# Expert gathers by token block, a hidden gate stage for block 0, and diagonals made by ScalarE, in a two-layer hybrid encoder on one Trainium2 core

## The reference

```python
x = x + _peer(_rmsnorm(x, norm_ffn[i]), peer_wq[i], peer_keys[i], peer_u[i], peer_v[i])
gate = jax.nn.sigmoid(_rmsnorm(x, norm_ple[i]) @ ple_gate[i])
x = x + (p[i] @ ple_proj[i]) * gate
```

```python
u = jnp.take(u_tab, ex, axis=0)
act = jax.nn.gelu(jnp.einsum('thkd,td->thk', u, hx), approximate=False) * gx
vv = jnp.take(v_tab, ex, axis=0)
return jnp.einsum('thk,thkd->td', act, vv)
```

## Time and profile before

| | us |
|---|---|
| median of 3 runs | 1844.28 |
| lowest and highest of them | 1842.87, 1846.96 |
| the profiled execution's own time | 1852.54 |
| its span in the profile | 1850.7 |
| its mean granted PE clock, as a share of full speed | 0.955 |
| PE busy | 1523.7 (82%) |
| DVE busy | 1339.5 (72%) |
| ACT busy | 439.3 (24%) |
| POOL busy | 568.6 (31%) |

### The profile page before, as it was taken

How to read it: one execution, slowest core, us unless ns; L and a number is a source line. 1 busy time by engine, 2 the same in 40 slices (tenths; PEclk the granted TensorE clock), 3 DMA queues, 4 the chain that set the end, 5 groups by cost and what they waited for, 6 DMA issues and landing times. The chain is left out here.

```text
span 1850.7 us, 23157 instructions
## 1 busy us (share of the span) xinstructions
PE 1523.7 (82%) x8613; PEld 849.1 (46%) x8613; DVE 1339.5 (72%) x3171; ACT 439.3 (24%) x1145; POOL 568.6 (31%) x556
## 2 busy tenths in 40 slices
PE   8999487979787887888899993878787887978886
PEld 7987342424333333422599872424333333423224
DVE  5776887877868587866477678777868696877654
ACT  5653211202111111100366441202111111201003
POOL 0010243434343433343000102434443443334321
PEclk9999799999999999999999996989899999999998
DMA  7312599999999999999242126999999999999980
GB/s 287 115 48 104 215 390 418 410 405 424 404 405 398 422 390 427 404 426 427 114 160 98 65 93 270 397 395 421 397 427 407 424 401 427 402 410 412 427 362 34
DMA packets 83767, 604.43 MB, mean 327 GB/s; under 512 B 9296, under 2 KB 9424, under 8 KB 10704
## 3 DMA queue, kind: packets, MB, share of 16 engines
q0 software_dynamic: 73728, 536.90, 70.2%
q1 hardware_dynamic: 9936, 66.21, 9.4%
HBM read 602.03 MB, written 1.05 MB: 326 GB/s over the span
## 5 line engine op out<-in xcount | busy, mean ns | idle before, releaser
L1480 PE MATMUL PS<-gath,diag 128*128 128x512 f32 x2048 | 1005.5, 631 | 285.5 <-DVE diag L1042 284.9
L1031 DVE CUSTOM_DVE_ANT_0 gath<-gath,xn 128x1024 f32<-128x1024 f32 x512 | 626.1, 1224 | 320.2 <-DMA gath<-in_experts,idx 319.9
L370 POOL DMA_INDIRECT gath<-in_experts,idx x512 | 535.0, 1045 | 842.5 <-PE PS L1480 779.9
L1480 PEld LDWEIGHTS PS<-gath,diag 128*128 128x128 f32 x2048 | 377.5, 197 | 878.7 <-DVE diag L1042 535.0
L615 ACT ACTIVATE hgel<-hid 128x1 f32<-128x1 f32 x512 | 103.9, 203 | 1088.3 <-DVE hid L1031 1088.3
L1136 PE MATMUL PS<-hTh,high 128*128 128x256 f32 x592 | 179.1, 303 | 5.2 <-DVE hTl L691 3.5
L1042 DVE TENSOR_SCALAR diag<-cst,hgel,gate 128x128 f32<-128x128 f32 x512 | 176.0, 344 | 0.0
L674 DVE TENSOR_TENSOR low<-ring,high 128x1024 fp32r<-128x1024 f32 x110 | 133.6, 1223 | 55.9 <-ACT high L390 55.7
L1136 PE MATMUL PS<-hTh,low 128*128 128x256 f32 x592 | 166.5, 281 | 0.0
L1136 PE MATMUL PS<-hTl,high 128*128 128x256 f32 x592 | 166.5, 281 | 0.0
L390 ACT CAST high<-ring 128x1024 fp32r<-128x1024 f32 x110 | 114.5, 1046 | 31.1 <-PE PS L1152 28.9
(11 more groups left out here) (241 smaller groups left out, 1339.2 us busy)
## 6 DMA issues: line engine op xcount, KB each, us to landing
ring<-in_w_slabs SPq DMA_DIRECT2D x58, 1024.0 KB, 5.2
gath<-in_experts,idx POOLq DMA_INDIRECT x512, 10.8
xres<-in_x SPq DMA_DIRECT2D x2, 512.0 KB, 4.6
gffn<-in_gain_ffn SPq DMA_DIRECT2D x2, 512.0 KB, 5.7
out<-obuf SPq DMA_DIRECT2D x2, 512.0 KB, 2.6
cst<-in_consts SPq DMA_DIRECT2D x1, 680.0 KB, 10.9
praw<-in_p_t SPq DMA_DIRECT2D x1, 512.0 KB, 15.5
gfin<-in_g_final SPq DMA_DIRECT2D x1, 512.0 KB, 3.1
```

Source lines behind the costliest of these rows:

```text
L370: pool.indirect_dma_start(gath[:, n % NB], None, experts[L], bass.IndirectOffsetOnAxis(ap=idx[:, h, tb, k:k + 1], axis=0)).then_inc(landed ...
L1031: dve.tensor_tensor_reduce(out=u, in0=u, in1=xn[:, tb], scale=1.0, scalar=0.0, op0=ALU.mult, op1=ALU.add, accum_out=hid[:, i:i + 1]).then_ ...
L1480: ins = mm(PS[:, 2 * tb + s], diag[:, n % ND], gath[:, n % NB, D + 512 * s:D + 512 * (s + 1)], start=i == tb * TOPK, stop=i == (PH - 1) * ...
```

## The change

The slots of a layer go block by block: 128 slots of block 0, all eight heads, and then 128 of block 1. A ranking is now one head of one block, 16 in a layer instead of 9, and stands between the slots of the ranking before (pieces after slots 2, 6, 10 and 14 of its 16). Only ranking 0 stands ahead of the first slot. The score tile is kept per block (`scA` for two heads of block 0, `scB` for all heads of block 1).

ACT makes the diagonals, one slot behind the Gelu, in two activations: the Gelu times the gate value (128x1), and the identity times that (128x128). `LAG` is gone.

The gate stage of block 0 stands between block 1's slots (`t` counts them): DVE adds the sums at slot 4, PE transposes at 5, ACT copies the rows out at 8, PE multiplies by one unsplit f32 row tile at each second slot from 10 to 24 (`gate_block0`), ACT takes the Sigmoids at 26, DVE multiplies and adds at 28, the next norm of block 0 (or its part of the output) follows at 30 to 40. After the last slot only block 1's half is left. In the order of ACT there, the split of the next layer's first weight tile stands ahead of the Sigmoids. The 16 warming matmuls on PE at the end of layer 0 are gone.

```diff
+T_SUM, T_RMS, T_GATE0, T_SIGMOID, T_NEXT = 4, 8, 10, 26, 30
+T_GSPLIT = (34, 40, 46, 52)
...
+                for tb in range(TB):
+                    for h in range(PH):
+                        pool.wait_ge(idx_ready, ranked_by(L, tb * PH + h))
+                        for k in range(TOPK):
+                            i = tb * SLOTS + h * TOPK + k
+                            n = TB * SLOTS * L + i
+                            if n >= NB:
+                                pool.wait_ge(spent, n - NB + 1)
+                            pool.indirect_dma_start(gath[:, n % NB], None, experts[L], bass.IndirectOffsetOnAxis(ap=idx[:, tb, h, k:k + 1], axis=0)).then_inc(landed[n % NB], 16)
+                            if i == SLOTS + T_RMS + NB:
+                                norm(3 * L + 2, (0,))
+                            if i == SLOTS + T_NEXT + NB + 2:
+                                norm(3 * L + 3, (0,))
+                norm(3 * L + 2, (1,))
+                norm(3 * L + 3, (1,))
...
+                def gelu(i):
+
+                    act.wait_ge(dot_made, TB * SLOTS * L + i + 1)
+                    act.activation(hgel[:, i % ND:i % ND + 1], hid[:, i:i + 1], ACT.Gelu).then_inc(gel_made, 1)
+
+                def weight(i):
+
+                    n, r, k = TB * SLOTS * L + i, i // TOPK, i % TOPK
+                    if k == 0:
+                        act.wait_ge(gate_ready, ranked_by(L, r))
+                    act.wait_ge(gel_made, n + 1)
+                    act.activation(hgel[:, i % ND:i % ND + 1], hgel[:, i % ND:i % ND + 1], ACT.Copy, scale=gate[:, r // PH, r % PH, k:k + 1]).then_inc(hid_gated, 1)
+                    if n >= ND:
+                        act.wait_ge(spent, n - ND + 1)
+                    act.wait_ge(hid_gated, n + 1)
+                    act.activation(diag[:, n % ND], ident, ACT.Copy, scale=hgel[:, i % ND:i % ND + 1]).then_inc(diag_made, 1)
...
+                for r in range(RANKINGS):
+                    for j in range(TOPK):
+                        i = r * TOPK + j
+                        gelu(i)
+                        if i:
+                            weight(i - 1)
+                        if r + 1 < RANKINGS and j == 10:
+                            exponentials(r + 1)
+                        if r + 2 < PH:
+                            if j in (6, 11):
+                                queries_out(2 * r + 4 + (j == 11))
+                            if j in (9, 14):
+                                scores_out(2 * r + 4 + (j == 14))
+                        t = i - SLOTS
+                        if t == T_SUM + 1:
+                            for n in range(2):
+                                half_square(3 * L + 2, n)
+                        if t == T_RMS:
+                            block0_rows()
+                        if t == T_SIGMOID:
+                            act.activation(stat[:, 220:221], minus_half, ACT.Sigmoid)
+                            sigmoids(0)
+                            act.activation(stat[:, 221:222], minus_half, ACT.Gelu)
+                        if t == T_NEXT:
+                            for n in range(2):
+                                half_square(3 * L + 3, n)
+                        if t in T_GSPLIT:
+                            split(projection_tile(L, "ple", 2 + T_GSPLIT.index(t)))
+                weight(TB * SLOTS - 1)
...
+                if L < DEPTH - 1:
+                    split(projection_tile(L + 1, "in", 0))
+                sigmoids(1)
...
-                def weight(n, i):
-
-                    if i % PAIRS == 0:
-                        dve.wait_ge(gate_ready, PH * L + i // PAIRS + 1)
-                    dve.wait_ge(gel_made, n + 1)
-                    if n >= ND:
-                        dve.wait_ge(spent, n - ND + 1)
-                    h, tb, k = i // PAIRS, i % PAIRS // TOPK, i % TOPK
-                    dve.tensor_scalar(diag[:, n % ND], ident, hgel[:, i:i + 1], gate[:, h, tb, k:k + 1], ALU.mult, ALU.mult).then_inc(diag_made, 1)
...
+                def peers_added(tb):
+
+                    dve.wait_ge(spent, SLOTS * (TB * L + tb + 1))
+                    for n in range(2):
+                        s = slice(n * 512, (n + 1) * 512)
+                        dve.tensor_tensor(xres[:, tb, s], xres[:, tb, s], PS[:, 2 * tb + n], ALU.add).then_inc(x_ready[tb], 1)
...
+                keys_ranked(0)
+                pairs_ranked(0)
+                experts_found(0)
...
+                for r in range(RANKINGS):
+                    for j in range(TOPK):
+                        i = r * TOPK + j
+                        dot(i)
+                        if r + 1 < RANKINGS:
                             if j == 2:
-                                keys_ranked(h + 1, both)
+                                keys_ranked(r + 1)
                             if j == 6:
-                                pairs_ranked(h + 1, both)
+                                pairs_ranked(r + 1)
                             if j == 10:
-                                experts_found(h + 1, both)
+                                experts_found(r + 1)
                             if j == 14:
-                                gates_made(h + 1)
-                        if j in (16, 26):
-                            m = 2 * h + 8 + (j == 26)
-                            if m < HC + 6:
+                                gates_made(r + 1)
+                        if j in (8, 13):
+                            m = 2 * r + 8 + (j == 13)
+                            if m < HC + 2:
                                 split(projection_tile(L, "wq", m) if m < HC else projection_tile(L, "ple", m - HC))
-                for i in range(PH * PAIRS - LAG, PH * PAIRS):
-                    weight(first_pair + i, i)
...
+                        t = i - SLOTS
+                        if t == T_SUM:
+                            peers_added(0)
+                        if t == T_SIGMOID + 2:
+                            gated_added(0)
+                        if t == T_NEXT + 4:
+                            if L < DEPTH - 1:
+                                normalized(3 * L + 3, 0)
+                            else:
+                                written(0)
+                        if t in T_GSPLIT:
+                            split(projection_tile(L, "ple", 2 + T_GSPLIT.index(t)))
+                peers_added(1)
...
+                def gate_block0(k):
+
+                    tile = projection_tile(L, "ple", 2 + k)
+                    if k == 0:
+                        pe.wait_ge(hT0_ready, KT * (L + 1))
+                    pe.wait_ge(filled[tile.slab % RING], 16 * fills(L, tile.slab))
+                    for n in range(2):
+                        ins = mm(PS[:, n], xT0[:, k], raw(tile.slab, tile.half)[:, n * 512:(n + 1) * 512],
...
+                def gate_block1():
+
+                    for k in range(KT):
+                        tile = projection_tile(L, "ple", 2 + k)
+                        pe.wait_ge(low_dve, tile.count + 1)
+                        b = tile.count % DEEP
+                        if k == 0:
+                            pe.wait_ge(hT_lo, KT * (3 * L + 3))
+                        if k == 0:
+                            pe.wait_ge(x_ready[1], 2 * (3 * L + 2))
+                        if k >= KT - 2:
+                            continue
+                        for c, (h, w) in enumerate(((hTh, high), (hTh, low), (hTl, high))):
+                            for n in range(2):
+                                ins = mm(PS[:, 2 + n], h[:, k, P:SEQ], w[:, b, n * 512:(n + 1) * 512], start=k == 0 and c == 0, stop=False)
+                        ins.then_inc(part_used, 1)
+                    for n in range(2):
+                        for k in (KT - 2, KT - 1):
+                            b = projection_tile(L, "ple", 2 + k).count % DEEP
+                            for c, (h, w) in enumerate(((hTh, high), (hTh, low), (hTl, high))):
+                                ins = mm(PS[:, 2 + n], h[:, k, P:SEQ], w[:, b, n * 512:(n + 1) * 512], start=False, stop=k == KT - 1 and c == 2)
+                            if n:
+                                ins.then_inc(part_used, 1)
+                        if n == 0:
+                            ins.then_inc(gate_ps, 1)
...
+                        t = i - SLOTS
+                        if t == T_SUM + 1:
+                            transposed(0)
+                        if T_GATE0 <= t < T_GATE0 + 2 * KT and (t - T_GATE0) % 2 == 0:
+                            gate_block0((t - T_GATE0) // 2)
+
+                pe.wait_ge(sgm_ready, 4 * L + 2)
+                pe.wait_ge(x_ready[0], 2 * (3 * L + 3))
+                transposed(1)
+                gate_block1()
```

361 lines of the change are left out of this document (176 added, 185 removed).

## The result

The changed kernel takes 1791.15 us (median of 4 runs, 1786.75 to 1792.76), the kernel before beside it on the same chip 1845.62 us (4 runs, 1842.87 to 1847.34). The ratio is 0.970, with a 95% interval of 0.968 to 0.9725: 54.5 us less, against a forecast of 1782 us and a range of 1763 to 1814. The profiled execution of the changed kernel took 1791.59 us by itself, with a span of 1789.5 us; the one before had 1852.54 and 1850.7. So the two profiled executions differ by 61.0 us: the one before stood 6.9 us above the median of its kernel, the one of the changed kernel at it.

What follows compares the result with a forecast made beforehand. The prediction took the slots to be bound by DMA, which lost 52.0 us. Its terms, -38 + 1.2 - 10 - 15.5 = -62.3 us, gave 1790.2 us against the profiled execution, 1782 us for the median; range 1763 to 1814.

Steps and rivals of the forecast that it cites:

- The lag: Slots: a diagonal waits for one further dot instead of two; landing to `spent` 6.8 us, slack up 2 us to about 7.
- The slots' size: Slots of both layers: 38 of the 52.0 us that DMA loses are won, with 1.2 us added for a moved load.
- the reserve of 7 us a layer: Slots: DMA loss left standing, 7 us a layer, for cold starts and boundaries where delays add up.
- PE is some 3 us late and recovers: Block 0's gate stage among the slots: 14 us of tiles and 2 us of transposes within 20 slots delay PE only briefly.
- The term of +1.2 us: Slots: layer 1's load of the last gain, 0.5 MB, moves into them and costs 1.2 us.
- ScalarE's diagonal: Slots: 0.4 us for the diagonal and 0.2 for the product on ACT, hidden in a slot of 2.456 us.
- Index numbers: Ranking boundaries, 15 a layer: gathers newly wait for numbers some 3.4 us late, without DMA cost given slack of 7.
- End of layer 0: Last dot to next layer's first matmul: 10 us less, 6.2 of it from the first gate matmul on (25.1 instead of 31.3).
- End of layer 1: Last dot to last output: four shorter steps, 5.8, 5.0, 11.3 and 6.2 us, together 15.5 us less.
- the slots did not keep their pace: Rival for the slots: late index numbers drain the queue at boundaries and eat all 52 us; 1820 us, chance 0.17.
- PE's clock did not fall in every pause: Rival for the slots: PE drops to 1.2 GHz in DVE's pauses, making the kernel 38 us slower, 1882 us; chance 0.07.
- The ends did not shrink by half: Rival for both layer ends: slower splits or slab, so they give 13 us instead of 25.5; 1794 us, chance 0.12.

Runs made afterwards that it cites:

- E1: Kernel before with the diagonal one slot behind the dot instead of two, still on VectorE: 1817.33 us, ratio 0.985.
- E3: Changed kernel with the diagonals back on VectorE, two slots behind the dot: 1824.86 us, ratio 0.988.
- E9: Changed kernel with the diagonals back on VectorE, one slot behind the dot: 1795.66 us, ratio 0.971.
- E5: Changed kernel with seven gather buffers instead of eight: 1832.49 us, ratio 0.991.
- E2: Kernel before, slots still head by head, with ScalarE making the diagonals one slot behind the Gelu: 1813.83 us, ratio 0.982.
- E8: Changed kernel with ranking pieces after slots 1, 4 and 7 instead of 2, 6 and 10: 1796.77 us, ratio 0.973.
- E7: Changed kernel with the Sigmoids of block 1 ahead of the split of the next layer's first tile: 1788.36 us, ratio 0.968.
- E11: Changed kernel with no diagonal lag, Sigmoids ahead of the next layer's split, and 36 warming matmuls before each layer's first slot: 1782.94 us, ratio 0.964.

## Why the prediction was right

The mechanism, the sign and all three places were right. The sum was -62.3 us; between the two profiled executions -61.2 came, between the medians -54.5. The closeness to -61.2 is partly luck: 4.6 us too much in the slots stand against 3.1 too little at the end of layer 1 and 1.2 ahead of the first gather, which had no term. By its own steps:

- **The lag.** Right, and nearly all of the slots' gain: E1, E3 and E9 each show some 16 us a layer for a slot of lag, and E5 takes it back with a buffer. From landing to `spent` I had 6.8 us. In the changed kernel a dot starts at 862.70 and PE's work on that slot at 867.32, which with 1.98 us for four matmuls is 6.6.

```profile
862.70 1.23 DVE L1099 CUSTOM_DVE_ANT_0 gath<-gath,xn 128x1024 f32<-128x1024 f32 x1 [1.19 <-DMA gath<-in_experts,idx]
```

```profile
866.87 0.40 ACT L641 ACTIVATE diag<-cst,stat 128x128 f32<-128x128 f32 x1
```

```profile
867.32 3.70 PE L1550 MATMUL PS<-gath,diag 128*128 128x512 f32 x8 [0.44 <-ACT diag L641]
```

- **The slots' size.** -38 + 1.2 = -36.8 was forecast, -32.2 came. Of the 52.0 us of DMA's loss 35.1 were won, not 38: the reserve of 7 us a layer was a little small (8.4 are lost), and its place was not the boundaries. In layer 0 some 2.6 us lie at the very end, when the last gathers land and none follows, and 0.6 in the first 10 us; no slack wins these, and the kernel before has them as well (1.9 us in its last 3.6), so the 52.0 held about 5 us that could not be won.

```profile
860.00:865.10 5.10, 4.17 (x9) 1.56 (x10) 2.47 (x4) 1.58 (x6) 0.00 (x0) 1.00 0.49 206
```

  The rest, about 5 us, lies in block 0's gate stage (1.2 us at 548 to 588, 2.9 at 588 to 630, 0.8 at 630 to 670), which I had taken as recovered within the slack. The step that failed is "PE is some 3 us late and recovers". PE came late, and at the low clock (3.66 us for four matmuls), into the tiles:

```profile
580.55 3.66 PE L1550 MATMUL PS<-gath,diag 128*128 128x512 f32 x4 [2.69 <-ACT diag L641]
```

  From there it waited for nothing until past 622, eight tiles of 1.88 us included: the tiles took the time in which it would have caught up. The sum itself showed it: 35 + 16 = 51 us of PE against 49 of DMA. The rest of the gap is bytes. The term of +1.2 us counted the load of the last gain; block 0's part of the output, another 0.5 MB, moved into the slots of layer 1 as well (SP's queue), and these two make 2.5 us. With the 35.1 that gives the 32.2 to within the rounding.

```profile
1531.94 0.34 SPq L328 DMA_DIRECT2D out<-xn  x1
```

- **ScalarE's diagonal.** The price of 0.4 us was right (402 ns), the product's 0.2 was 280 ns, and both are hidden. The Trainium skill, "ScalarE: Activation LUTs", section "Rules for kernel authors", would leave this multiplication to VectorE. Per instruction the rows bear it out (0.344 us there, 0.402 here, and 0.280 more for the product). In the time they don't: ACT had room for it, DVE's dot stands ahead of every release, and with the diagonal on DVE the slots are 3.4 us a layer longer (E1 against E2, E9 against the change). In the medians that shows between E1 and E2 (3.5 us); between E9 and the change it is inside the intervals.
- **Index numbers.** Right that they cost nothing. Their waits between the slots (80 us over 28) looked like a new bound; DMA stood at 423 to 428 GB/s through them, and E8 took them away without gain.
- **End of layer 0.** -10 forecast, -10.9 measured (46.1 us from the last dot to the next layer's first matmul before, 35.2 after). From the gate's first matmul on it was 25.3 us against my 25.1, by two errors that cancel: the Sigmoids began at 16.8 us and not 14.5, since the gate's first seven pairs of matmuls ran at the low clock (2.7 us, see E7) and the four splits wait for them; and from there to the first matmul it took 8.5 us instead of 10.6. The term "1.5 for a cold PE since the warming is gone" had a wrong ground, as the warming is still there. A cold PE came all the same, from the wait for the slab: after 3.58 us idle at 898.29 the next layer's first matmul takes 0.55 us, against 0.35 before, and the front of layer 1 up to its first gather takes 196.6 us (900.31 to 1096.93) against 194.8 before (929.79 to 1124.64). In E7, where that wait is short and the first matmul takes 0.36 us, it is 194.0. These 1.8 us are what I had put down as 1.5, one stage later; over all runs that front takes 194.9 to 197.0 us where the layer's first matmul took 0.55 us and 193.0 to 195.1 where it took 0.36, so the 2 us are a mean.
- **End of layer 1.** -15.5 forecast, -18.6 measured: 1.0 us less in the step to the gate than worked out, 0.7 less after the Sigmoids, and 1.2 less between the two, since PE was at its full clock there, where I had put the first matmuls at the low one. The two ends had the clocks the wrong way round, by no rule that the trace shows.
- **The median.** The step that missed most in the stated time, 9 us. The 52.0 us of DMA's loss, and with it the whole sum, were read from an execution that stood 8.3 us above its median (6.9 by the four runs), and I subtracted the sum as it was from the median. After's profiled execution stands at its median (1791.59 against 1791.15). Medians differ by 54.5 us, profiled executions by 61.0, so a usual execution of the kernel before had less to win. The extra time of the profiled one probably lay in its slots: outside them it took 500.3 us, and E2 and E1, the same order in executions within 1 us of their medians, 500.8 and 495.9. Then a usual execution loses some 45 to 50 us of DMA time and not 52, and the slots gave 25 to 30. A second trace of the kernel before would be needed to show it.

The rivals: the slots did not keep their pace (421 and 422 GB/s, and almost no loss at the boundaries outside the gate stage). PE's clock did not fall in every pause (0.96 over the slots). Single falls are there: over the first 50 us of slots, which begin with PE's wait for the first diagonal, it is 0.82. This agrees with the Trainium skill, "TensorE: Matmul & The Clock Gate", Part 1, which lets PE fall after an idle stretch, but E11 shows that it costs nothing here. The ends did not shrink by half: they gave 27.8 us (9.2 + 18.6) where the forecast had 25.5.
